# Attention values product with queries on the PSUM partitions, softmax scale applied when the product leaves PSUM, and an expert scatter by an unweighted one-hot

## The reference

```python
def one_block(args):                       # attention, 8 heads, value width 64
    i, qb = args
    s = jnp.einsum('bqhd,bkhd->bhqk', qb, k, ...) * scale
    s = jnp.where(key_pos[None, :] <= q_pos[:, None], s, -jnp.inf)
    p = jax.nn.softmax(s, axis=-1).astype(v.dtype)
    return jnp.einsum('bhqk,bkhv->bqhv', p, v)

def moe_ffn(h, w_router, w_e_gate, w_e_up, w_e_down):
    logits = jnp.einsum('bsd,de->bse', h, w_router, ...)
    top_vals, top_idx = lax.top_k(logits, TOP_K)
    top_w = jax.nn.softmax(top_vals, axis=-1)
    combine = jnp.sum(jax.nn.one_hot(top_idx, N_EXPERTS) * top_w[..., None], axis=-2)
    for e in range(N_EXPERTS):
        y = y + combine[..., e:e + 1] * swiglu(h, w_e_gate[e], w_e_up[e], w_e_down[e])
```

## Time and profile before

| | |
|---|---|
| median of 3 runs | 1165.09 us (1164.87 to 1167.19) |
| the profiled execution's own time | 1167.5 us |
| its span, first to last instruction | 1165.8 us |
| PE busy | 1100.5 us, 94% |
| weight loads (PEld) busy | 942.7 us, 81% |
| DVE busy | 823.7 us, 71% |
| ACT busy | 669.9 us, 57% |
| mean granted TensorE clock | 0.976 |

### The profile page before, as it was taken

How to read it: one execution, slowest core, us unless ns; L and a number is a source line. 1 busy time by engine, 2 the same in 40 slices (tenths; PEclk the granted TensorE clock), 3 DMA queues, 4 the chain that set the end, 5 groups by cost and what they waited for, 6 DMA issues and landing times.

```text
span 1165.8 us, 16875 instructions
## 1 busy us (share of the span) xinstructions
PE 1100.5 (94%) x6535; PEld 942.7 (81%) x6535; DVE 823.7 (71%) x1110; ACT 669.9 (57%) x956; POOL 73.9 (6%) x119
## 2 busy tenths in 40 slices
PE   4999999988999998999999996999999999999997
PEld 3979777778999997979787775888888888788885
DVE  3577766875545545457866776689898888989885
ACT  3567655454434435457755553576767676677763
POOL 4001430000000000000521000000000000000000
PEclk9999999998999999999999996799999999999999
DMA  5553354465446444345344454499899898999992
GB/s 180 202 181 118 116 174 145 145 215 202 161 170 239 153 163 151 101 145 181 102 161 144 147 193 166 142 322 339 301 324 365 290 346 307 381 305 349 342 327 90
DMA packets 147670, 250.19 MB, mean 215 GB/s; under 512 B 5166, under 2 KB 108676, under 8 KB 147588
## 3 DMA queue, kind: packets, MB, share of 16 engines
q1 hardware_dynamic: 145808, 246.89, 61.6%
q10 hardware_dynamic: 1780, 2.19, 0.6%
HBM read 248.02 MB, written 1.05 MB: 214 GB/s over the span
## 4 chain that ended last, share of the span: by engine, by line
PE 82%; DVE 10%; ACT 4%; issue 2%; POOL 1%; DMA 1%; ACTq 0%; DVEq 0%; POOLq 0%
PE PS L622 26%; PE PS L1077 9%; PE PS L1078 9%; PE PS L1079 9%; PE PS L938 5%; PE PS L940 5%; PE PS L939 5%; DVE w_lo L402 4%; PE PS L1048 2%; PE PS L710 2%; DVE m_lo L1759 2%; PE PS L648 1%; PE PS L1036 1%; ACT w_hi L393 1%; PE PS L805 1%
## 5 line engine op out<-in xcount | busy, mean ns | idle before, releaser
L402 DVE TENSOR_TENSOR w_lo<-ring,w_hi 128x1536 fp32r<-128x1536 f32 (+1 forms) x192 | 311.6, 1633 | 126.4 <-ACT w_hi L393 125.9
L393 ACT ACTIVATE w_hi<-ring 128x1536 fp32r<-128x1536 f32 (+1 forms) x192 | 264.8, 1388 | 152.5 <-PE PS L940 85.8
L1759 DVE TENSOR_TENSOR m_lo<-ring,m_hi 128x512 fp32r<-128x512 f32 (+2 forms) x256 | 185.7, 754 | 91.9 <-ACT m_hi L1275 90.2
L1275 ACT ACTIVATE m_hi<-ring 128x512 fp32r<-128x512 f32 (+2 forms) x256 | 157.5, 631 | 141.7 <-PE PS L622 139.1
L1077 PE MATMUL PS<-w_hi,hTe 128*96 128x384 f32 (+1 forms) x384 | 131.5, 342 | 0.7 <-issue 0.7
L622 PE MATMUL PS<-m_hi,h_hi 128*128 128x512 f32 (+2 forms) x352 | 125.2, 356 | 2.1 <-DVE m_lo L1759 2.1
L1078 PE MATMUL PS<-w_hi,hTe 128*96 128x384 f32 (+1 forms) x384 | 124.5, 324 | 0.0
L1079 PE MATMUL PS<-w_lo,hTe 128*96 128x384 f32 (+1 forms) x384 | 124.5, 324 | 0.0
L622 PE MATMUL PS<-m_lo,h_hi 128*128 128x512 f32 (+2 forms) x352 | 120.5, 342 | 0.0
L622 PE MATMUL PS<-m_hi,h_lo 128*128 128x512 f32 (+2 forms) x352 | 120.5, 342 | 0.0
L938 PE MATMUL PS<-h_hi,w_hi 128*128 128x256 f32 x352 | 100.6, 286 | 0.8 <-DVE h_lo L1741 0.8
(11 more groups left out here) (320 smaller groups left out, 2197.6 us busy)
## 6 DMA issues: line engine op xcount, KB each, us to landing
ring<-in_w_in_dram SPq DMA_DIRECT2D x40, 1024.0 KB, 5.1
ring<-in_w_exp_gate_dram SPq DMA_DIRECT2D x24, 1536.0 KB, 7.8
ring<-in_w_exp_up_dram SPq DMA_DIRECT2D x24, 1536.0 KB, 9.2
ring<-in_w_exp_down_dram SPq DMA_DIRECT2D x24, 1536.0 KB, 8.5
ring<-in_w_branch_dram SPq DMA_DIRECT2D x12, 1024.0 KB, 4.9
ring<-in_w_ffn_gate_dram SPq DMA_DIRECT2D x6, 1536.0 KB, 6.5
ring<-in_w_ffn_up_dram SPq DMA_DIRECT2D x6, 1536.0 KB, 7.1
ring<-in_w_ffn_down_dram SPq DMA_DIRECT2D x6, 1536.0 KB, 6.4
```

What stands on the lines that cost most here:

```text
L393: act.activation(split_parts(u, j)[0], ring[:, i % NSLOT, w0:w0 + words], ACT.Copy)\
L402: dve.tensor_tensor(lo, ring[:, (j // 2) % NSLOT, w0:w0 + words], hi.bitcast(F32), SUB).then_inc(sem(f"lo_ready{b}"), 1)
L1275: act.activation(hi, raw, ACT.Copy).then_inc(sem("m_hi_ready"), 1)
L1759: dve.tensor_tensor(lo, raw, hi.bitcast(F32), SUB).then_inc(sem("m_lo_ready"), 1)
```

## The change

In the attention, `scaled` goes away. `turn` transposes the unscaled exponentials. `values` takes the transposed probabilities as the stationary operand and the 64 value columns as the moving one, so that queries are on the output partitions: three matmuls for each head in place of two. DVE multiplies with the inverse sums when it empties the bank (`attended`), into `yA_tok`. Then PE transposes back, 8 transposes a layer (`turn_a`), and ACT and DVE write the high and low parts straight from PSUM (`ya_high`, `ya_low`), in place of `values` on ACT, `y_high(0)` and `y_low(0)`. Two bank uses a layer are added.

In the expert part `wsel` goes away. The bare one-hot is transposed to `selT`, now fp32r. `rows_out` writes the result rows as `ye_hi` (ACT) and `ye_lo` (DVE), `scatter` is two fp32r matmuls a chunk in place of a float32 one, and DVE multiplies by the router weight as it adds. The router weights themselves (`weigh`) are computed by DVE ahead of expert 1, no longer ahead of the first gather.

```diff
                 def turn(h):
                     bank, full = begin(L, f"pt{h}")
-                    pe.wait_ge(sem("p_ready"), H * L + h + 1)
+                    pe.wait_ge(sem("exp_done"), H * L + h + 1)
@@ values, PE
-                        o = bank[j * DV:(j + 1) * DV, 0:T]
-                        pe.matmul(o, vt[:, 0, h * DV:(h + 1) * DV], PT[:, j, 0:T], start=True, stop=False)
-                        mm = pe.matmul(o[:, P:T], vt[:, 1, h * DV:(h + 1) * DV], PT[:, j, T:3 * P], start=False, stop=True)
+                        near_keys, far_keys = (vt[:, b, h * DV:(h + 1) * DV] for b in range(2))
+                        o = [bank[:, (2 * a + j) * DV:(2 * a + j + 1) * DV] for a in range(TT)]
+                        pe.matmul(o[0], PT[:, j, 0:P], near_keys, start=True, stop=True)
+                        pe.matmul(o[1], PT[:, j, P:2 * P], near_keys, start=True, stop=False)
+                        mm = pe.matmul(o[1], PT[:, j, 2 * P:3 * P], far_keys, start=False, stop=True)
@@ new, PE, between gate(7) and near(4)
+                def turn_a():
+                    for a in range(TT):
+                        bank, full = begin(L, f"ya{a}")
+                        pe.wait_ge(sem("ya_tok_ready"), KB * (L + 1))
+                        for i in range(KB):
+                            mm = pe.transpose(bank[:, i * P:(i + 1) * P], yA_tok[:, a, 2 * i:2 * i + 2, :], ident[:, :])
+                        mm.then_inc(full, 1)
@@ scatter, PE
-                    pe.matmul(PS[:, 4 + b, :], selT[:, e, a * P:(a + 1) * P], ye[:, d * 512:(d + 1) * 512],
-                              start=True, stop=True).then_inc(sem(f"aux_full{b}"), 1)
+                    rows, w = selT[0:CAP, e, a * P:(a + 1) * P], slice(d * 512, (d + 1) * 512)
+                    pe.matmul(PS[:, 4 + b, :], rows, ye_hi[0:CAP, w], start=True, stop=False)
+                    pe.matmul(PS[:, 4 + b, :], rows, ye_lo[0:CAP, w], start=False, stop=True).then_inc(sem(f"aux_full{b}"), 1)
@@ DVE, attention
-                def scaled(h):
-                    dve.wait_ge(sem("exp_done"), H * L + h + 1)
-                    step(dve.reciprocal(mx[:, h % 2, :], sums[:, h % 2, :]))
...
+                def attended(i):
+                    w = slice(2 * i, 2 * i + 2)
+                    dve.wait_ge(sem("exp_done"), H * L + 2 * i + 2)
+                    step(dve.reciprocal(sums[:, w, :], sums[:, w, :]))
+                    bank, free = full(L, f"o{i}")
+                    dve.tensor_tensor(yA_tok[:, :, w, :], bank[:, 0:T].rearrange("p (a j c) -> p a j c", a=TT, j=2),
+                                      sums[:, w, :].rearrange("p j a -> p a j").unsqueeze(3).broadcast_to([P, TT, 2, DV]), MUL)\
+                       .then_inc(free, 1)
@@ DVE, experts
             def rows_out(n):
-                wait_used(dve, expert_unit(n), HALVES - 1)
-                dve.tensor_copy(ye[:, 512:1024], PS[0:CAP, 7, :]).then_inc(sem("ye_dve"), 1)
+                for c in range(2):
+                    w = slice(c * 512, (c + 1) * 512)
+                    dve.wait_ge(sem("ye_hi_ready"), 2 * n + c + 1)
+                    dve.tensor_tensor(ye_lo[0:CAP, w], PS[0:CAP, 6 + c, :], ye_hi[0:CAP, w].bitcast(F32), SUB)\
+                       .then_inc(sem("ye_lo_ready"), 1)
@@ added
-                    dve.tensor_tensor(x, x, PS[:, 4 + b, :], ADD).then_inc(sem(f"aux_free{b}"), 1)
+                    dve.scalar_tensor_tensor(x, PS[:, 4 + b, :], wt[:, a, e - 1:e], x, MUL, ADD).then_inc(sem(f"aux_free{b}"), 1)
@@ one_pass
                 if isinstance(r, int):
-                    weigh()
+                    most_rows()
                 dve.wait_ge(sem("psel_ready"), 2 * (r + 1))
-                for a in range(TT):
-                    dve.tensor_tensor(wsel[:, a], psel[:, a].bitcast(F32), wt[:, a, :].unsqueeze(2).broadcast_to([P, NE, CAP]), MUL)\
-                       .then_inc(sem("sel_ready"), 1)
...
                 for e in range(NE):
+                    if e == 1 and isinstance(r, int):
+                        weigh()
                     expert(r, e, n + e)
```

More of the change, by code:

```diff
@@ L1489, in turned, with ya_high @@
                     act.activation(PT[:, h % 2, :], bank[:, 0:3 * P], ACT.Copy).then_inc(free, 1)
-                def values(i):
-                    bank, free = full(L, f"o{i}")
-                    act.activation(ys[:, i, :], bank[:, 0:T], ACT.Copy).then_inc(free, 1)
+                def ya_high(a):
+                    bank, _ = full(L, f"ya{a}")
+                    act.activation(y_parts[0][0][:, :, a * P:(a + 1) * P], bank.rearrange("p (k t) -> p k t", t=P), ACT.Copy)\
+                       .then_inc(sem("ya_hi_ready"), 1)
                 def pool_out(i):
@@ L1502, in mixer @@
                 gate(0), exps(0), exps(1), upper_exp(2), lower_exp(2), gate(1), turned(0), turned(1), exps(2), exps(3)
[L1503 to L1506, removed]
+                gate(2), turned(2), turned(3), exps(4), exps(5), upper_exp(3), lower_exp(3)
+                gate(3), turned(4), turned(5), exps(6), exps(7), upper_exp(4), lower_exp(4)
+                gate(4), turned(6), turned(7), pool_out(0), pool_out(1), gate(5)
+                gate(6, 5), gate(7, 6), ya_high(0), ya_high(1), gate(8, 7), gate(9, 8), gate(10)
                 for i in range(2):
@@ L1611, in expert @@
                                 wait_aux_full(act, b, uses)
[L1612 removed]
+                                act.activation(selT[0:CAP, 2 * c:2 * c + 2, :], two(PS[0:CAP, 4 + b, :]), ACT.Copy)\
                                    .then_inc(sem(f"aux_free{b}"), 1)
@@ L1901, in masked, with ya_low @@
                                                  ADD, MIN, nbs[:, h % 2, a:a + 1]).then_inc(free if a else sem("nb_ready"), 1)
-                def scaled(h):
-                    dve.wait_ge(sem("exp_done"), H * L + h + 1)
-                    step(dve.reciprocal(mx[:, h % 2, :], sums[:, h % 2, :]))
-                    for a, w in ((0, slice(0, P)), (1, slice(P, 3 * P))):
-                        ins = dve.tensor_scalar(Pr[:, h % 3, w], Pr[:, h % 3, w], mx[:, h % 2, a:a + 1], None, MUL)
-                        if a == 0:
-                            step(ins)
-                    ins.then_inc(sem("p_ready"), 1)
-                    dve.wait_ge(sem("p_ready"), H * L + h + 1)
+                def attended(i):
[6 more added lines that the diff above has]
+                       .then_inc(free, 1)
+                    freed(L, f"o{i}")
+                    dve.engine_nop().then_inc(sem("ya_tok_ready"), 1)
+                def ya_low(a):
+                    bank, free = full(L, f"ya{a}")
+                    hi, lo = (y[:, :, a * P:(a + 1) * P] for y in y_parts[0])
+                    dve.wait_ge(sem("ya_hi_ready"), 2 * L + a + 1)
+                    dve.tensor_tensor(lo, bank.rearrange("p (k t) -> p k t", t=P), hi.bitcast(F32), SUB).then_inc(free, 1)
                 split(L, "g1", LAST)
                 masked(0), masked(1)
-                scaled(0), scaled(1)
                 split(L, "g2")
@@ L1951, in mixer @@
                 longer(2), to_end(3)
-                scaled(2), scaled(3)
                 split(L, "g3")
+                attended(0)
                 masked(4), masked(5)
                 longer(3), to_end(4)
-                scaled(4), scaled(5)
                 split(L, "g4")
+                attended(1)
                 masked(6), masked(7)
                 longer(4)
-                scaled(6), scaled(7)
                 split(L, "g5")
+                attended(2)
                 split(L, "g6")
-                near(0), near(1), to_end(5), longer(5)
+                near(0), near(1), attended(3), to_end(5), longer(5)
                 split(L, "g7")
@@ L1966, in mixer @@
                 split(L, "g8")
+                ya_low(0), ya_low(1)
                 near(4), near(5), to_end(7), longer(7)
```

45 lines of the change are left out of this document (21 added, 24 removed).

## The result

Six runs of the changed kernel have a median of 1160.63 us (1157.60 to 1161.48), six of the kernel before beside them 1167.22 us (1164.87 to 1167.72): a ratio of 0.9942, with a 95% interval of 0.9931 to 0.9953. The change makes the kernel 6.6 us faster, 0.6%. The profiled span went from 1165.8 to 1159.7 us. The forecast was 1159.4, with a range of 1153.8 to 1163.9.

The account below looks back on a forecast made before the run. PE was taken to bound the kernel. Mixers +4.55, scatter -10.9, losses +2.5 and router -1.8 sum to -5.65 us, applied to the median of 1165.09: 1159.4 us, range 1153.8 to 1163.9.

Parts of the forecast that it names:

- Values: Attention values product: 12 records a pair of heads at 0.109 us, +0.50 us a pair, +4.0 us for eight.
- rival A: Values records advance at streaming speed, 0.055 us, giving -1.2 in place of +4.0: 1154.2 us; chance 0.13.
- `scaled` removed: Attention: PE gets back its waits for the scaling on DVE, one in each layer, -1.2 us.
- Scatter: Experts: each part falls from 1.72 to 0.94 us of PE, 0.78 saved, -10.9 us for 14 parts.
- Banks: Experts: PE waits at the second scatter part for DVE's additions, 0.2 us an expert, +1.2 us for six.
- Weights: Small router-weight instructions on DVE ahead of expert 1 delay it: +1.3 us there, 1.1 more than elsewhere.
- Router: Behind the router, PE's wait for DVE's first copy of gathered tokens goes, -1.8 us.
- Last scatter: End of kernel: start 1.1 us later, products 2 us shorter, DVE's additions then set the pace; -0.2 to +0.3, counted 0.
- B: Values loads don't hide at all, 0.163 us a record, +9.2 in place of +4.0: 1164.6 us; chance 0.04.
- C: Clock rises some 3 us sooner because the gathers run without the hole, sparing 1.5 us: 1157.9; chance 0.10.
- D: DVE becomes the bound of the expert loop, scatter's gain lost, +8.0: 1173; chance 0.06.
- E: Experts: three times the forecast stall, 0.6 more an expert, or slower `added`: +4 to +5, about 1163.7; chance 0.12.

Follow-up runs that it names:

- attention alone: Kernel before with only the attention part of the change, expert part as it was: 1169.69 us, ratio 1.0027.
- weights in another gap: Changed kernel with the router-weight instructions moved on DVE from in front of expert 1 into a gap in expert 0: 1160.86 us in one run.
- experts alone: Kernel before with only the expert part of the change, attention as it was: 1159.21 us, ratio 0.9938.
- 128-column stream: Changed kernel with 128 value columns streamed in each values matmul instead of 64, DVE picking each head's half: 1161.22 us, ratio 0.9960.
- Second part later: Changed kernel with the second part of each scatter one half of an expert later: 1156.68 us in one run.
- combined kernel: Kernel before with changed expert part, scaling moved earlier on DVE, router weights in expert 0, second scatter part later, last scatter waiting per half: 1154.89 us, ratio 0.9904.

## Why the prediction was right, point by point

The change was forecast at -5.65 us and measured at -6.1 by the spans and -6.6 by the medians. The forecast time, 1159.4, was set from a median before of 1165.09 us from three runs; with six it is 1167.22, so the 1160.63 measured lies above the forecast although the gain was larger.

**Values, forecast +4.0.** Right in mechanism and size. A record takes 0.111 us (0.109 forecast) and a pair 1.29 us, +0.48, or +3.8 for eight. In the layer's stretch part of that is not seen: after, it takes 68.76 us (533.65 to 602.41) against 67.19 without scaling in the old form, +1.57 for four pairs, +3.1 in both layers. The chains of the two show where the other 0.35 a layer goes. What stands behind a pair is 0.14 us shorter in the new form (the six turns 0.67 us against 0.81, three times, and the gate product behind the last pair 5.54 against 5.68), which gives back 0.56; and the last pair, behind products of the linear attention, takes 1.48 us and not 1.29. So the term was the right one and read too narrowly: a pair is to be priced with the matmuls behind it. The Trainium skill's formula N/2.4 + 2.5 ns ("TensorE: Matmul & The Clock Gate", section "Back-to-back issue gap"), which the prediction names for rival A, gives 29 ns at 64 columns and not A's 0.055 us; the trace shows neither.

**Transposes back, +1.75.** Right: 0.87 us a layer on PE's chain.

**`scaled` removed, -1.2.** This is the mis-sized term. Removing it gives -2.4. The wait was the right one, that of the turns for the multiplies, but the list of waits has only 0.6 us of it a layer: from start to start the turns of heads 2 and 3 lose 0.87 us and those of heads 4 and 5 another 0.32. With it, +3.1 + 1.75 - 2.4 = +2.5, which the starts of the router product bear out: 2.38 in attention alone, 2.74 in the changed kernel.

**Scatter, -10.9.** Right: a part fell from 1.72 to 0.92 us, 0.80 (forecast 0.78).

**Banks, +0.2 an expert.** The place and the cause were right (the first addition ends as PE arrives), the size was not: 0.39 us, as 1.60 saved less 1.21 kept shows too. It comes to 1.1 us more in six experts. Moving the part later takes back half of the 0.39.

**Weights, +1.1 at expert 1 beyond the others.** Measured 0.9 (1.21 - 0.31), in the wait of 0.74 us for `x_tok` and by "weights in another gap".

**Router, -1.8.** Measured -1.98, and no wait in the gathers.

**Last scatter, 0 (-0.2 to +0.3).** Wrong, +1.0 us, outside its bounds. The wait grew from 0.83 to 2.00 us as forecast (+1.1). The products should have won most of that back; but the clock fell behind the wait: it was 0.50 from 1151.4 us on, and the second part's matmuls start 0.42 us apart instead of 0.23. In the kernel before, it stayed at 1.00. From the first of these matmuls to the end of the span it is 9.88 us, and was 10.08. In "experts alone" the clock fell a chunk later, and the same takes 9.40.

**The rivals.** A and B fell with the 128-column stream. C did not hold: the clock rose 3.25 us after the first expert matmul, 3.87 before, a gain of 0.3 us, and in other profiles of the same stage it rose later than before. D was far off: DVE is busy 88.94 of 100 us in the middle of the experts, and the period fell. E in part, with the bank waits at twice the forecast (E's "three times my stall, 0.6 more" is a slip: three times is 0.4 more, and 0.6 more is what its +4 to +5 rests on).

So the sizes off were, against the change, the banks (+1.1) and the last scatter (+1.0), and for it `scaled` (-1.2) and the values (-0.9). They nearly cancelled, and the forecast of -5.65 came to within 1 us of the measured -6.6. The total being right proves little about the terms; the stages do.

## What to carry to other kernels

Before an output is turned around on TensorE, count the columns of the stationary operands: here a float32 record with 128 of them took 0.111 us with 64 or with 128 columns streamed, and the old form, with two 64-column operands in different halves of the array, took 0.81 us a pair where one behind the other took 1.45. When work is removed from an engine's queue, price the wait for it from start to start of the instructions that wait, since the list of waits had half of it; and try moving the work earlier first, which here gave the same without the new form. In a sum over repeated stages, read the period between two occurrences of one instruction, which shows 0.2 us where the run's time does not.

## What the runs showed of the hardware

Two programs with the same instructions up to a point reached it up to 4.4 us apart, and 3.3 us of that is TensorE's clock. The same 42 records of branch products in each layer take 9.83 us, or 11.43 us when the clock is at half for part of them. The chain of waits of the kernel before:

```profile
222.60 11.43 PE PS L622 x42
...
667.16 9.83 PE PS L622 x42
```

and of the changed kernel:

```profile
224.21 9.83 PE PS L620 x42
...
668.53 11.43 PE PS L620 x42
```

In both kernels and both layers PE stands idle for 2.18 us just ahead of these records, and in each profile the clock fell behind only one of the two: to 0.50 from 224 to 226 us before, to 0.51 from 670 to 672 after, the 1.2 GHz level. "Second part later" had no such dip, and the combined kernel had two and was still the fastest. So the same idle time is followed by a fall in one layer and not in the other, and what decides it I can't say. After the first expert matmul, which follows the sparse stretch of the router, the clock had gone from 1.2 to 2.4 GHz after 3.18 us in one profile (128 columns streamed) and 6.06 us in another (second part later), with the same work before and behind. At the lower level the expert matmuls start 0.32 us apart and at the higher 0.175, so each microsecond of it costs nearly half a microsecond. So a single profiled span carries 1.6 us or more either way, and a term below that is read from its own stage.
